# Attention output with V stationary: two pairs of heads in the column halves of TensorE, and the result turned back

## The reference

```python
# DSA: per query the 128 best keys by an index score, one latent key and value for all heads
p = masked_softmax(s, dist >= 0);  o = einsum('bthk,btkd->bthd', p, vs)
# NSA: 2 KV heads, 4 query heads each; selected blocks (here all), a window (here all), and compressed keys
o_slc = einsum('btgqnl,btgnld->btgqd', p, vs)
o_win = einsum('btgqs,bsgd->btgqd', p_w, vw)
o = g0 * o_cmp + g1 * o_slc + g2 * o_win
merged = sigmoid(gate_a) * (o_a @ w_up_a) + sigmoid(gate_b) * (o_b @ w_up_b)
x = x + merged @ w_out
x = x + square(relu(rms_norm(x) @ w_ff1)) @ w_ff2
```

## Time and profile before

| | |
|---|---|
| median of 3 runs | 803.83 us (802.96 to 803.85) |
| the profiled execution | 802.97 us, of which the span 801.2 us |
| granted TensorE clock, mean | 0.998 |
| TensorE, matmuls | 787.4 us, 98% of the span |
| TensorE, weight loads | 679.9 us, 85% |
| VectorE | 434.7 us, 54% |
| ScalarE | 354.2 us, 44% |
| GpSimd | 76.3 us, 10% |
| DMA | 88 GB/s over the span |

### The profile page before, as it was taken

The page is one execution under the profiler, slowest core; times in us unless marked ns, Lnnn a source line. Parts: engine busy times, 40 slices in busy tenths (PEclk is TensorE's granted clock), DMA queues, the critical chain, the costliest instruction groups (busy, mean ns, idle before and its releaser), DMA issues.

```text
span 801.2 us, 11070 instructions
## 1 busy us (share of the span) xinstructions
PE 787.4 (98%) x4193; PEld 679.9 (85%) x4193; DVE 434.7 (54%) x854; ACT 354.2 (44%) x683; POOL 76.3 (10%) x109
## 2 busy tenths in 40 slices
PE   8999999999999999999999999999999999999998
PEld 8988988889889888888788888888888888888886
DVE  4479867777689938674765433333334423323323
ACT  7666265555466676543534333333333322322320
POOL 3030311100113221100002200000000000000000
PEclk9999999999999999999999999999999999999999
DMA  9522121111011121101253222232233233233232
GB/s 336 204 74 64 53 80 54 54 29 51 1 54 54 38 68 54 54 27 53 84 206 105 87 99 86 98 106 91 93 106 97 87 106 101 83 106 103 83 103 106
DMA packets 21396, 70.86 MB, mean 88 GB/s; under 512 B 2400, under 2 KB 2784, under 8 KB 21088
## 3 DMA queue, kind: packets, MB, share of 16 engines
q1 hardware_dynamic: 21200, 70.13, 26.8%
q10 hardware_dynamic: 144, 0.02, 0.0%
HBM read 68.05 MB, written 2.10 MB: 88 GB/s over the span
## 4 chain that ended last, share of the span: by engine, by line
PE 88%; DVE 8%; ACT 1%; issue 1%; DMA 1%; SPq 0%; DVEq 0%; ACTq 0%
PE psum L1382 24%; PE psum L1384 24%; PE psum L1383 24%; PE psum L1557 5%; PE psum L1390 5%; PE psum L1538 2%; PE psum L1539 1%; DVE w_lo L1024 1%; DVE score L1218 1%; DVE prob L1209 1%; PE psum L1509 1%; DVE top L1217 1%; DMA stage<-in_panels 1%; DVE x2T L1364 1%; ACT g L963 1%
## 5 line engine op out<-in xcount | busy, mean ns | idle before, releaser
L1024 DVE TENSOR_TENSOR w_lo<-stage,w_hi 128x1024 fp32r<-128x1024 f32 (+4 forms) x150 | 147.0, 983 | 237.5 <-ACT w_hi L774 237.1
L774 ACT ACTIVATE w_hi<-stage 128x1024 fp32r<-128x1024 f32 (+4 forms) x150 | 125.7, 843 | 168.8 <-DMA stage<-in_panels 168.6
L1382 PE MATMUL psum<-hT_hi,w_hi 128*128 128x512 f32 x384 | 156.8, 408 | 0.0
L1384 PE MATMUL psum<-hT_hi,w_lo 128*128 128x512 f32 x384 | 150.1, 391 | 0.0
L1383 PE MATMUL psum<-hT_lo,w_hi 128*128 128x512 f32 x384 | 149.8, 390 | 0.0
L1382 PE MATMUL psum<-a_hi,w_hi 128*128 128x512 f32 x256 | 99.6, 389 | 0.0
L1383 PE MATMUL psum<-a_lo,w_hi 128*128 128x512 f32 x256 | 99.6, 389 | 0.0
L1384 PE MATMUL psum<-a_hi,w_lo 128*128 128x512 f32 x256 | 99.6, 389 | 0.0
L1384 PEld LDWEIGHTS psum<-hT_hi,w_lo 128*128 128x128 f32 x384 | 72.1, 188 | 15.5
L1383 PEld LDWEIGHTS psum<-hT_lo,w_hi 128*128 128x128 f32 x384 | 72.4, 189 | 12.3
L1382 PEld LDWEIGHTS psum<-hT_hi,w_hi 128*128 128x128 f32 x384 | 72.5, 189 | 12.2
(11 more groups left out here) (229 smaller groups left out, 1240.9 us busy)
## 6 DMA issues: line engine op xcount, KB each, us to landing
stage<-in_panels SPq DMA_DIRECT2D x104, 512.0 KB, 3.5
xT_in<-in_xT SPq DMA_DIRECT2D x8, 256.0 KB, 5.2
x_in<-in_x SPq DMA_DIRECT2D x4, 512.0 KB, 8.3
phi<-in_phi SPq DMA_DIRECT2D x2, 1024.0 KB, 6.2
x2T<-in_xT SPq DMA_DIRECT2D x1, 2048.0 KB, 9.2
out_xT<-x2T SPq DMA_DIRECT2D x8, 256.0 KB, 2.0
stage<-in_panels SPq DMA_DIRECT2D x4, 408.0 KB, 3.1
stage<-in_panels SPq DMA_DIRECT2D x4, 384.0 KB, 4.1
```

The costliest lines, as they stand in the source:

```text
L774: return nc.scalar.activation(dst, src, ACT.Copy, scale=scale)
L1024: tt_op(w_lo[:, p % SLOTS, cols], stage[:, p % SLOTS, cols], w_hi[:, p % SLOTS, cols].bitcast(F32), ALU.subtract)\
L1382: mm(dst, a_h, b_h, start=start, stop=False)
L1384: return mm(dst, a_l, b_h, start=False, stop=stop)
```

## The change

- `probT` grows to two slots of four heads each. For a token block and key block a slot holds the heads in the order 0, 2, 1, 3 of the group, so that heads 0 and 1 of a slot lie beside each other as 256 moving columns for one half, and the others for the other half.
- `pv` is now one step for four heads (24 steps instead of 96), at the end of every fourth turn. Per key block it issues two float32 matmuls: V (128 keys by 64 channels) stationary, 256 columns of probabilities moving, one writing PSUM partitions 0 to 63 and the other 64 to 127. The result is transposed: channels by tokens.
- After 8 heads a new step `take` (ScalarE, right behind `exp(u)` in turn u = 12, 20, ..., 92, and once behind the loop) copies the bank to `o_raw`; a new step `turn` (TensorE, in the same turn, ahead of the last atom) transposes its four 128x128 blocks back into the same bank; `close` comes one turn later than before (13, 21, ...) and reads that.
- The compressed attention's steps come one turn later. `TAIL` becomes 2, 3, 3 with `turn` and `close` of the last tile behind the first 2. `o_a` shrinks to two tiles, so its `close` waits for the `oT` of two tiles ago. Some buffers lie elsewhere. `qa_scale` on GpSimd waits for the last `cmpPT`.

```diff
+    TAKEN_AT = H + PV_LAG
...
-        s0 = (tt + 1) * H + PV_LAG + 1
+        s0 = tt * H + TAKEN_AT + 2
...
-        if u > PV_LAG and (u - PV_LAG) % H == 0:
-            step("close", (u - PV_LAG) // H - 1)
+        if u >= TAKEN_AT and (u - TAKEN_AT) % H == 0:
+            step("take", (u - TAKEN_AT) // H)
+        if u > TAKEN_AT and (u - TAKEN_AT) % H == 1:
+            step("close", (u - TAKEN_AT) // H)
...
+        if u >= TAKEN_AT and (u - TAKEN_AT) % H == 0:
+            step("turn", (u - TAKEN_AT) // H)
         fill(1, now=u)
-        if u >= PV_LAG:
-            step("pv", u - PV_LAG)
+        if u >= PV_LAG and (u - PV_LAG) % G == G - 1:
+            step("pv", (u - PV_LAG) // G)
...
+                elif kind == "take":
+                    ti, = a
+                    ps = wait_full(se, ("O", ti))
+                    drained(copy(o_raw[:, :], ps), ("O", ti))
...
+                    for u in range(n * G, (n + 1) * G):
+                        wait_drained(te, ("PT", u))
+                    dst = psum[:, bank[("O", n // 2)][0], half * 2 * P:(half + 1) * 2 * P]
                     for j in range(tt + 1):
...
-                        last = mm(dst, probT[:, u % 2, j * P:(j + 1) * P], v, start=j == 0, stop=j == tt)
+                        for c in range(2):
+                            last = mm(dst[c * DH:(c + 1) * DH], v,
+                                      probT[:, n % 2, j, 2 * c:2 * c + 2, :].rearrange("p i t -> p (i t)"),
+                                      start=j == 0, stop=j == tt)
...
+                elif kind == "turn":
+                    ti, = a
+                    wait_drained(te, ("O", ti))
+                    transposes(("turn", ti), [o_raw[:, k * P:(k + 1) * P] for k in range(4)])
...
-                    ps = wait_full(ve, ("O", ti))
+                    ps = wait_full(ve, ("turn", ti))
```

More of the change, by code:

```diff
@@ L75 @@
 SIGMOID_FILL = 10
-TAIL = 3, 5
+TAIL = 2, 3, 3
 WARM = 22
@@ L250, in hybrid_layer @@
             fill(SIGMOID_FILL, now=u)
+        if u >= TAKEN_AT and (u - TAKEN_AT) % H == 0:
+            step("turn", (u - TAKEN_AT) // H)
         fill(1, now=u)
-        if u >= PV_LAG:
-            step("pv", u - PV_LAG)
-    step("close", NU // H - 1)
+        if u >= PV_LAG and (u - PV_LAG) % G == G - 1:
+            step("pv", (u - PV_LAG) // G)
+    step("take", NU // H - 1)
     last_mix = late.pop(NU + PV_LAG, [])
@@ L260, in hybrid_layer @@
     fill(TAIL[0])
+    step("turn", NU // H - 1)
+    step("close", NU // H - 1)
+    fill(TAIL[1])
     step("oT", 0, TT - 1)
     step("oT_low", 0, TT - 1)
-    fill(TAIL[1])
+    fill(TAIL[2])
     step("sigmoid", 0)
@@ L312, in hybrid_layer @@
         elif kind in ("cmpS", "cmpPT", "cmpO", "kc", "kcT", "kwT", "qaT", "oT"):
-            ti = max(unit_of_step[(kind, *a)] - PV_LAG - 1, 0) // H
-            bank.use((kind, *a), rings["O"][(ti + 1) % 2])
+            ti = max((unit_of_step[(kind, *a)] - TAKEN_AT - 2) // H, -1)
+            bank.use((kind, *a), rings["O"][ti % 2])
         elif kind == "pT":
             use_ring("PT", ("PT", a[0]))
-        elif kind == "pv" and a[0] % H == 0:
-            use_ring("O", ("O", a[0] // H))
+        elif kind == "pv" and a[0] % 2 == 0:
+            use_ring("O", ("O", a[0] // 2))
+        elif kind == "turn":
+            bank.use(("turn", a[0]), bank[("O", a[0])][0])
         elif kind == "tile" and a[1] == 0:
@@ L463, in hybrid_layer @@
         score = place("score", [P, 9 * P], Z + 95 * K)
-        prob = place("prob", [P, PROBS, S], Z + 100 * K)
-        probT = place("probT", [P, 2, S], Z + 108 * K)
+        probs = [place(f"prob{i}", [P, S], Z + k * K) for i, k in enumerate((100, 102, 120, 122))]
+        probT = place("probT", [P, 2, TT, G, P], Z + 104 * K)
+        o_raw = place("o_raw", [P, H * DH], Z + 55 * K)
         square = place("square", [P, TT * H * DH], Z + 100 * K)
@@ L576, in wait_released, with wait_pv, probT_of @@
                 wait_full(eng, what)
-        def wait_pv(eng, u):
-            if u % H == H - 1:
-                wait_full(eng, ("O", u // H))
-            else:
-                eng.wait_ge(pv_done, u + 1 - u // H)
+        def wait_pv(eng, n):
+            if n % 2:
+                wait_full(eng, ("O", n // 2))
+            else:
+                eng.wait_ge(pv_done, n // 2 + 1)
+        def probT_of(u):
+            h = units[u][2] % G
+            return probT[:, u // G % 2, 0:units[u][1] + 1, h % 2 * 2 + h // 2, :]
         def panel_part(p, part):
@@ L1293, in _ @@
                     if br == WIN:
-                        weigh(ve, link, tt, ps, inv, ("O", ti))
+                        weigh(ve, link, tt, ps, inv, ("turn", ti))
                     else:
[L1296 to L1300, removed]
+                        o = o_a[:, tt % 2, :] if br == DSA else o_b[:, tt, :]
+                        if br == DSA and tt >= 2:
+                            wait_full(ve, ("oT", 0, tt - 2))
+                        drained(tt_op(o.rearrange("p (h d) -> p h d", d=DH), ps.rearrange("p (h d) -> p h d", d=DH),
+                                      inv[:, :, None].to_broadcast([P, H, DH]), ALU.mult), ("turn", ti))
+                        wait_drained(ve, ("turn", ti))
                 elif kind == "oT_low":
@@ L1542, in _ @@
                     te.wait_ge(exp_done, u + 1)
-                    transposes(("PT", u), [prob[:, u % PROBS, j * P:(j + 1) * P] for j in range(units[u][1] + 1)])
+                    transposes(("PT", u), [probs[u % PROBS][:, j * P:(j + 1) * P] for j in range(units[u][1] + 1)])
                 elif kind == "pv":
[L1545 to L1548, removed]
+                    n, = a
+                    br, tt, h0 = units[n * G]
@@ L1549, in _ @@
+                    half = n % 2
+                    if half == 0:
+                        open_bank(("O", n // 2))
                         if br == SLC:
                             wait_drained(te, ("proj", C_KV2, tt))
-                    wait_drained(te, ("PT", u))
-                    dst = psum[:, bank[("O", u // H)][0], h * DH:(h + 1) * DH]
+                    for u in range(n * G, (n + 1) * G):
+                        wait_drained(te, ("PT", u))
+                    dst = psum[:, bank[("O", n // 2)][0], half * 2 * P:(half + 1) * 2 * P]
@@ L1558, in _ @@
-                    if h == H - 1:
-                        full(last, ("O", u // H))
+                        for c in range(2):
+                            last = mm(dst[c * DH:(c + 1) * DH], v,
+                                      probT[:, n % 2, j, 2 * c:2 * c + 2, :].rearrange("p i t -> p (i t)"),
+                                      start=j == 0, stop=j == tt)
+                    if half:
+                        full(last, ("O", n // 2))
                     else:
                         last.then_inc(pv_done, 1)
+                elif kind == "turn":
+                    ti, = a
+                    wait_drained(te, ("O", ti))
+                    transposes(("turn", ti), [o_raw[:, k * P:(k + 1) * P] for k in range(4)])
@@ L1611, in _ @@
                     m, tt = a
-                    wait_drained(te, ("O", 2 * TT + tt if m == 0 else TT + tt))
-                    transposes(("oT", m, tt), [(o_b if m else o_a)[:, tt, k * P:(k + 1) * P] for k in range(4)])
+                    wait_drained(te, ("turn", TT + tt if m else 2 * TT + tt))
+                    o = o_b[:, tt, :] if m else o_a[:, tt % 2, :]
+                    transposes(("oT", m, tt), [o[:, k * P:(k + 1) * P] for k in range(4)])
                 elif kind == "tile":
```

31 lines of the change are left out of this document (18 added, 13 removed).

## The result

The changed kernel takes 812.53 us, the median of four runs (811.83 to 813.24); the kernel before, run on the same chip, takes 803.39. The ratio is 1.0114, 95% interval 1.0096 to 1.0131: slower by 9.1 us. The prediction was 811 us. The profiled execution is 813.24 us with a span of 811.5, 10.3 above the span of before.

A forecast was written before the change was run, and what follows sets the result against it. TensorE was taken as the bound, so its work and added waits count in full: work -8.2, waits +15.7 and +1.4, given back -2, sum +6.9 us, forecast 811 us. The 8-in-10 range was 796 to 830.

The forecast's parts named there:

- Removed: Old `pv` matmuls on TensorE: 480 records of 0.111 us go, -53.3 us.
- New matmuls: New `pv` steps on TensorE: 240 records whose halves overlap only partly, in order of issue, +34 us.
- side by side: Rival for the new `pv` matmuls: halves overlap fully, 26.0 us, entering and leaving free; 797 us in all, chance 0.13.
- a step of tt 3 of 1.8 us: Sign in the profile after: a `pv` step this long, instead of about 2.2 us, would show the prediction wrong.
- Switching: TensorE entering and leaving the column halves: 0.12 us each, 48 times, +5.8 us, bounds 0 and 9.6.
- Turns: The `turn` steps on TensorE: 48 full transposes at 0.11 us, +5.3 us.
- The wait for `take`: TensorE at `turn` waits for ScalarE's copy behind `exp(u)`: mean 1.43 us, eleven turns, +15.7 us, bounds 10 and 22.5.
- The wait for `o_a`: TensorE's `oT` of DSA's third tile waits for `close` in turn 93: +1.4 us, bounds 0 and 2.4.
- Given back: TensorE's existing 6.8 us of waits: those on VectorE can shrink when TensorE comes later, -2 us.
- The clock: Rival: the new waits bring TensorE's granted clock down five times more, +9 us, 820 us in all, chance 0.08.

The follow-up runs named there:

- e2: The changed kernel with each `pv` step doing all key blocks of the first column half, then all of the second: 820.44 us.
- e7: The changed kernel with each `pv` step alternating the column halves every two key blocks: 813.54 us.
- e1: The changed kernel with `take` as the first step of its turn instead of behind `exp(u)`: 797.55 us.
- e6: e5 with the compressed attention's last three steps one turn later and `oT` of DSA's third tile in turn 94 instead of 93: 812.91 us.
- e8: e1 with the compressed attention's last three steps one turn later and `oT` of DSA's third tile in turn 94 instead of 93: 799.47 us.
- e9: e8 with the query transposes of turns 53, 61 and 69 one turn earlier: 796.88 us.
- e10: e9 with the fourth tile's last three compressed attention steps put back to turns 42 to 44: 790.93 us.
- e5: e1 with the query transposes of turns 45, 53, 61 and 69 one turn later: 814.83 us.
- e4: The changed kernel with `pv` at full width, 128 columns of V and no column halves, output not the layer's: 828.31 us.

## Why the prediction was right, and where not

The time came out 1.5 us above the forecast, from terms that erred both ways.

- **Removed.** The 480 records are gone, -53.3. Read over the whole stretch, as above, before's steps cost 0.11 us a record too.
- **New matmuls, the step that failed.** The prediction chose +34 on the ground that "a queue that keeps its order can only overlap the second record of one half with the first of the other". It does more (e2, e7): the halves run fully side by side, 26.0 us of streams. The prediction named a step of tt 3 of 1.8 us as a sign that it is wrong; the step takes 1.88, not 2.2, and speaks for the rival "side by side".
- **Switching.** 8.4 us against +5.8, within the bounds of 0 and 9.6, and against that same rival, which had it free: by the prediction's own reckoning that rival is faster only while streams and switches stay under 32.9 us, and they are 34.4. Going in, with the first pair, costs 0.15 us and coming out 0.20, where 0.12 was taken for each.
- **Turns.** 0.35 and 0.09 on the matmul behind, twelve times, 5.3: right. TensorE's work thus fell by 53.3 - 26.0 - 8.4 - 5.3 = 13.6 us, not 8.2.
- **The wait for `take`.** Eleven times, 13.9 us listed and 1.8 unlisted, 15.7 against +15.7. Its reading from before's times held in each of the four turns (1.0, 1.5, 1.2 and 1.9 us in turns 12, 60, 84 and 92, against 1.0, 1.4, 1.2 and 2.05), and its cause is shown by e1.
- **The wait for `o_a`.** 1.2 and 0.16 against +1.4. A turn's delay of `oT` removed it (e6).
- **Given back, -2: wrong in sign.** The waits other than these two went from 7.5 to 12.5 us, +5.0. They were set down as a reserve that a later TensorE would use up. But four of the query transposes, from which `q_st` is made, use the other bank than before, and the `pv` that opens it comes two turns later. The steps of the compressed attention all moved by one turn, so `cmp_e` stands as far ahead of its user as before, and its waits still went from 0.5 to 3.6 us. What is new there is that three of four turns have no `pv`, so that TensorE comes to them sooner; no run separates that. e6, e8 and e9 show what takes such waits away, one turn more between step and user, not why they grew.
- **The clock.** The prediction gave its fall a rival of its own, with five more; between the two profiled executions there is one more, 1.7 us. Between the kernels no difference shows: the changed one's executions have mean clocks of 0.996 to 0.998, those of before in the first series of experiments (fifteen) 0.995 to 1.000.
- **The sum.** -13.6 + 20.1 of listed waits + 2.1 for the thirteen additional ones + 1.7 = +10.3, against +10.3 of the span. The same sum in e10 is -13.6 + 2.1 + 0.3 = -11.2, against -11.8.

With the forecast's waits and the measured work the change would have cost 15.1 - 13.6 = 1.5 us; the waits for VectorE and the clock made it slower by as much as was said. The work was forecast 5.4 us too dear and the waits 7.1 too cheap, so the right size was in part luck; the right sign rests on the wait for `take`, without which (e1) the change is faster.

## What to carry to other kernels

When steps of several engines are laid out in turns, look for each TensorE step at what it needs and at who used its bank last: where that stands in the same turn it paid 0.7 to 5 us here. First place in the other engine's turn, or one turn more between the two, took most of that away (`take` 13.9 to 1.0 us, `q_st` 2.8 to 0, `cmp_e` 2.8 to 1.3). Each moved step must be looked at in its new turn as well: e5 and e8 made new waits that were longer than the old ones. A copy of a result long finished belongs ahead of the work that the turn itself begins. And two column halves are worth using even in short steps, if about 0.35 us for each visit is put into the sum.

## What the runs showed of the hardware

- Two float32 matmuls in the two column halves start 7 ns apart in the changed kernel and each pair takes the time of one (0.216 us for 256 columns), at every step. The Trainium skill, "TensorE: Matmul & The Clock Gate", section Measured speedup vs the span model, has about 4 ns for a further tile; the trace agrees but for 3 ns.
- A matmul whose half is idle starts ahead of up to four others (e2, e7; inferred from the starts, since no record names its half).
- A visit to the column halves costs 0.35 us: 0.10 going in, 0.05 in the first pair, 0.10 behind the last pair and 0.10 between the two matmuls that follow. At full width (e4) the same steps cost their streams and no more.
- The wait of 4.9 us in e9 was followed by a stretch at 1.2 GHz, and e5, with three waits over 4 us, had four more such stretches than e1. Shorter waits say little: the changed kernel has 13.9 us of waits for `take` and two stretches in the profiled execution, e4 13.3 us and none. Executions of one kernel differ too: before ranges from a mean clock of 0.995 at 804.4 us to 1.000 at 801.8.
